# Block 2's norm behind the output projection: sums taken inside the projection, one low part on VectorE

## What is computed

```
mix = concat([a_out, b_out]) @ w_o[i]
x   = layer_norm(ALPHA * x + mix, ln1_g[i], ln1_b[i])      # the norm of this case
gate, up = split(x @ w_ffn_in[i], 2)
ple = (p[i] @ w_ple[i]) * sigmoid(x @ w_ple_gate[i])
...
def layer_norm(x, g, b):
    mu  = mean(x, -1)
    var = mean(square(x - mu), -1)
    return (x - mu) * rsqrt(var + 1e-5) * g + b
```

## Time and profile before

| | |
|---|---|
| median of 3 runs | 2500.24 us (2498.78 to 2500.97) |
| the profiled execution, its own time | 2500.13 us |
| its span, first to last instruction | 2498.3 us |
| mean granted TensorE clock | 0.992 of full |
| PE busy | 2424.8 us, 97% of the span |
| PE weight loads busy | 2033.0 us, 81% |
| DVE busy | 1765.1 us, 71% |
| ACT busy | 1095.0 us, 44% |
| POOL busy | 1065.5 us, 43% |
| chain that ended last | PE 75%, DVE 10%, issue 5%, ACT 4%, POOL 3%, DMA 3% |

### The profile page before, as it was taken

One profiled execution on the slowest core, in us unless ns is written; L12 is line 12 of the kernel. 1 busy time (PEld: TensorE's weight loads), 2 busy tenths in 40 slices (PEclk: granted clock), 3 DMA queues, 4 the chain that ended last, 5 costly groups with the idle time before them and its releaser, 6 DMA issues.

```text
span 2498.3 us, 35167 instructions
## 1 busy us (share of the span) xinstructions
PE 2424.8 (97%) x13615; PEld 2033.0 (81%) x13615; DVE 1765.1 (71%) x2671; ACT 1095.0 (44%) x1803; POOL 1065.5 (43%) x600
## 2 busy tenths in 40 slices
PE   6999999999999999999999999999999999999997
PEld 4777788988777788998777779999877777999985
DVE  4677777864477787774597478887468747888746
ACT  4325532434426543443444555444444355444442
POOL 0323553434234244544254446544515534755441
PEclk8999999999999999999999999999999999999998
DMA  8613345553322433332232113332223212333221
GB/s 288 203 51 123 114 152 169 189 164 110 95 85 85 135 118 119 102 102 85 86 85 76 55 64 127 108 104 92 95 82 85 76 51 68 102 124 105 94 87 49
DMA packets 239645, 268.87 MB, mean 108 GB/s; under 512 B 19976, under 2 KB 204024, under 8 KB 239224
## 3 DMA queue, kind: packets, MB, share of 16 engines
q1 hardware_dynamic: 239480, 266.63, 33.1%
HBM read 264.51 MB, written 2.10 MB: 107 GB/s over the span
## 4 chain that ended last, share of the span: by engine, by line
PE 75%; DVE 10%; issue 5%; ACT 4%; POOL 3%; DMA 3%; SPq 1%; ACTq 0%; DVEq 0%; POOLq 0%
PE bank L2801 22%; PE bank L2803 22%; PE bank L2802 22%; DVE k_lo L2057 1%; DMA raw<-in_w_ffn_in 1%; DVE r L1908 1%; POOL w_lo L1652 1%; POOL k_lo L1663 1%; DMA raw<-in_ffn_w 1%; ACT k_hi L1105 1%; DVE u_sum L2074 1%; PE bank L3404 1%; PE bank L3470 1%; DVE u_t_raw L2087 1%; PE bank L3130 1%
## 5 line engine op out<-in xcount | busy, mean ns | idle before, releaser
L1663 POOL TENSOR_TENSOR k_lo<-raw,k_hi 128x512 fp32r<-128x512 f32 x297 | 430.0, 1459 | 542.9 <-ACT k_hi L1105 541.9
L1652 POOL TENSOR_TENSOR w_lo<-raw,w_hi 128x2048 fp32r<-128x2048 f32 x53 | 248.8, 4694 | 525.3 <-ACT w_hi L1051 446.3
L1105 ACT ACTIVATE k_hi<-raw 128x512 fp32r<-128x512 f32 x444 | 270.9, 626 | 310.7 <-PE bank L2803 249.4
L2801 PE MATMUL bank<-h_hi,k_lo 128*128 128x256 f32 (+1 forms) x1156 | 370.8, 321 | 3.8 <-DVE k_lo L2057 2.5
L2802 PE MATMUL bank<-h_lo,k_hi 128*128 128x256 f32 (+1 forms) x1156 | 369.6, 320 | 0.0
L2803 PE MATMUL bank<-h_hi,k_hi 128*128 128x256 f32 (+1 forms) x1156 | 369.5, 320 | 0.0
L2801 PE MATMUL bank<-h_hi,w_lo 128*128 128x512 f32 x800 | 325.0, 406 | 10.7 <-DVE h_lo L2017 3.9
L2803 PE MATMUL bank<-h_hi,w_hi 128*128 128x512 f32 x800 | 313.4, 392 | 0.0
L2802 PE MATMUL bank<-h_lo,w_hi 128*128 128x512 f32 x800 | 313.3, 392 | 0.0
L2801 PE MATMUL bank<-f_hi,k_lo 128*128 128x512 f32 x704 | 278.4, 395 | 8.6 <-DVE u_row L2118 2.9
L2801 PE MATMUL bank<-u_t_hi,k_lo 128*128 128x256 f32 x1008 | 282.6, 280 | 1.2 <-POOL k_lo L1663 1.2
(11 more groups left out here) (401 smaller groups left out, 4929.6 us busy)
## 6 DMA issues: line engine op xcount, KB each, us to landing
raw<-in_ffn_w SPq DMA_DIRECT2D x56, 1024.0 KB, 5.4
raw<-in_w_ffn_in SPq DMA_DIRECT2D x44, 1024.0 KB, 5.1
raw<-in_w_in SPq DMA_DIRECT2D x34, 1024.0 KB
b_raw<-in_ada_w SPq DMA_DIRECT2D x32, 1024.0 KB, 5.2
f_raw<-in_w_ffn_out SPq DMA_DIRECT2D x24, 512.0 KB, 3.4
z_a<-in_ada_w SPq DMA_DIRECT2D x4, 2048.0 KB, 14.1
g_raw<-in_ada_w SPq DMA_DIRECT2D x8, 1024.0 KB, 5.6
raw<-in_w_out SPq DMA_DIRECT2D x8, 1024.0 KB
```

The lines of the kernel that those rows point to most:

```text
L1105: act.activation(hi, src, ACT.Copy).then_inc(s.f_hi.up, 1)
L1652: pool.tensor_tensor(b.w_lo[p][:, 0:n], b.raw[p][:, 0:n], b.w_hi[p][:, 0:n].bitcast(F32), ALU.subtract)\
L1663: pool.tensor_tensor(lo, src, hi.bitcast(F32), ALU.subtract).then_inc(s.f_lo.up, 1)
L2801: pe.matmul(out, wlo, xhi, start=start, stop=False)
```

## The change

- Inside `attended(0)`, behind its first k, PE sums tiles 0 and 1 of x over the width into bank 6: two f32 matmuls. DVE (`dve_early_shift`) then subtracts this sum over 256 from all eight tiles, before the projection is added to them. What is left is a small mean.
- ACT squares tiles 0 to 6 as they become ready (`act_square_out`), ahead of its split(15); DVE squares tile 7. PE sums the squares of tiles 0 to 3 into bank 7 inside `attended(1)`, ahead of output tile 7, and those of tiles 4 to 6 at the start of `pe_layer_norm`. Then come the two sums of x as before, and the square of tile 7.
- The variance is now the mean of squares minus the square of the remaining mean: ACT squares bank 6, DVE subtracts (signal `s.var`). ACT's logarithm and exponential follow.
- Weight unit 15's low part moves from POOL to DVE, behind that subtraction.
- DVE takes the remaining mean off tiles 0 and 1 before the multiplications and off tiles 2 to 7 between them.
- The dummy matmuls ahead of `lay.pair(7)` are 8 in place of 19. Elsewhere they stay 19.

```diff
 def act_layer_norm(act, e, l):
-    for k in range(KD):
-        act.wait_ge(*s.ld(l, k + 1))
-        act.activation(b.sq[:, k, :], b.x[:, k, :], ACT.Square).then_inc(s.lsq.up, 1)
     act.wait_ge(*s.lmean(l, 2))
-    act.activation(b.r[:, :], bank[7][:, :], ACT.Ln, bias=b.eps[:, 1:2], scale=1.0 / D).then_inc(s.l_r.up, 1)
-    act.wait_ge(*s.l_r(l, 1))
+    act.activation(b.sq[:, 1, :], bank[6][:, :], ACT.Square, scale=1.0 / D).then_inc(s.l_r.up, 1)
+    act.wait_ge(*s.var(l, 1))
+    act.activation(b.r[:, :], b.sq[:, 1, :], ACT.Ln, bias=b.eps[:, 1:2]).then_inc(s.l_r.up, 1)
+    act.wait_ge(*s.l_r(l, 2))
     act.activation(b.r[:, :], b.r[:, :], ACT.Exp, scale=-0.5).then_inc(s.l_r.up, 1)
+def act_square_out(act, e, l, ks):
+    for k in ks:
+        act.wait_ge(*s.res(l, k + 1))
+        act.activation(b.sq[:, k, :], b.x[:, k, :], ACT.Square).then_inc(s.lsq.up, 1)
@@ ACT's program
     split(14)
+    act_square_out(act, e, l, range(KD - 1))
     split(15)
@@ POOL's program
     split(14)
-    split(15)
@@ DVE's program
-def dve_layer_norm(dve, e, l):
-    dve.wait_ge(*s.lmean(l, 1))
-    for k in range(KD):
-        dve.scalar_tensor_tensor(b.x[:, k, :], bank[6][:, :], -1.0 / D, b.x[:, k, :], ALU.mult, ALU.add)\
-           .then_inc(s.ld.up, 1)
-    dve.wait_ge(*s.l_r(l, 2))
+def dve_layer_norm(dve, e, lay, l):
+    dve.wait_ge(*s.res(l, KD))
+    dve.tensor_tensor(b.sq[:, KD - 1, :], b.x[:, KD - 1, :], b.x[:, KD - 1, :], ALU.mult).then_inc(s.lsum.up, 1)
+    dve.wait_ge(*s.l_r(l, 1))
+    dve.wait_ge(*s.lmean(l, 3))
+    dve.scalar_tensor_tensor(b.sq[:, 1, :], bank[7][:, :], 1.0 / D, b.sq[:, 1, :], ALU.mult, ALU.subtract)\
+       .then_inc(s.var.up, 1)
+    dve_split(dve, e, lay.pair(7))
+    for k in range(2):
+        dve_less_mean(dve, e, k, -1.0 / D)
+    dve.wait_ge(*s.l_r(l, 3))
     for k in range(KD):
-        dve.wait_ge(*s.ld(l, k + 1))
+        dve.wait_ge(*s.ld(l, KD + k + 1))
         dve_scaled(dve, e, k)
         if k == 0:
             dve_normed(dve, e, l * 2, 0)
+        if k + 2 < KD:
+            dve_less_mean(dve, e, k + 2, -1.0 / D)
         if k == 1:
             dve_normed_low(dve, e, l * 2, 0)
+def dve_early_shift(dve, e, lay, l):
+    dve.wait_ge(*s.lmean(l, 1))
+    for k in range(KD):
+        dve.wait_ge(*lay.bank_out(k % 2, PART_USE[k]))
+        dve_less_mean(dve, e, k, -1.0 / (2 * P))
@@ PE's program
 def pe_layer_norm(pe, e, l):
+    pe_square_sums(pe, e, l, range(4, KD - 1))
     pe.wait_ge(*s.lsum(l, 6))
+    pe.wait_ge(*s.ld(l, KD))
     pe.matmul(bank[6][:, :], b.ones[:, :], b.r[:, :], start=True, stop=False)
     pe.wait_ge(*s.res(l, KD))
     pe.matmul(bank[6][:, :], b.ones[:, :], b.x[:, KD - 1, :], start=False, stop=True).then_inc(s.lmean.up, 1)
-    for k in range(KD):
+    pe.wait_ge(*s.lsum(l, 7))
+    pe.matmul(bank[7][:, :], b.ones[:, :], b.sq[:, KD - 1, :], start=False, stop=True).then_inc(s.lmean.up, 1)
+def pe_square_sums(pe, e, l, ks):
+    for k in ks:
         pe.wait_ge(*s.lsq(l, k + 1))
-        op = pe.matmul(bank[7][:, :], b.ones[:, :], b.sq[:, k, :], start=(k == 0), stop=(k == KD - 1))
-    op.then_inc(s.lmean.up, 1)
+        pe.matmul(e.bank[7][:, :], b.ones[:, :], b.sq[:, k, :], start=(k == 0), stop=False)
@@ attended(0), inside the loop over k
+                if k == 0:
+                    for n in range(2):
+                        pe.wait_ge(*lay.bank_out(n, PART_USE[n]))
+                        op = pe.matmul(bank[6][:, :], b.ones[:, :], b.x[:, n, :], start=(n == 0), stop=(n == 1))
+                    op.then_inc(s.lmean.up, 1)
@@ attended(1), inside the loop over m
+                if m == 6:
+                    pe_square_sums(pe, e, l, range(4))
@@ the first pair of products behind the norm
-                  + [(bank[2], s.res(l, 4)), (bank[3], s.res(l, 4))])
+                  + [(bank[2], s.res(l, 4)), (bank[3], s.res(l, 4))], busy=BUSY_SHIFTED)
```

More of the change, by code:

```diff
@@ L32 @@
 NB = T // P
-BUSY = 19
+BUSY, BUSY_SHIFTED = 19, 8
 G = 256
@@ L590, in __init__ @@
         self.mh, self.mh2 = in_turn("mh_mh2", 8, 8)
-        self.gn_sq, self.lsq = in_turn("gn_sq_lsq", 2, 8)
+        self.gn_sq, self.lsq = in_turn("gn_sq_lsq", 2, 7)
         self.cn_sq, self.is_relu = in_turn("cn_sq_is_relu", 2, 9)
@@ L598, in __init__ @@
         self.gn_m, self.v_m = in_turn("gn_m_v_m", 2, 1)
-        self.gn_x, self.lsum = in_turn("gn_x_lsum", 2, 6)
+        self.gn_x, self.lsum = in_turn("gn_x_lsum", 2, 7)
         self.cn_x, self.wi = in_turn("cn_x_wi", 2, 1)
@@ L639, in __init__ @@
         self.v_n = up("v_n", 4)
-        self.lmean = up("lmean", 2)
-        self.ld = up("ld", 8)
-        self.l_r = up("l_r", 2)
+        self.lmean = up("lmean", 3)
+        self.ld = up("ld", 2 * KD)
+        self.l_r = up("l_r", 3)
         self.n2_sum = up("n2_sum", 3 + 6)
@@ L646, in __init__ @@
         self.n2_r = up("n2_r", 3)
-        self.n2_var = up("n2_var", 1)
+        self.var = up("var", 2)
         self.lxr = up("lxr", KD + 1)
@@ L2445, in dve_layer_norm, with dve_less_mean @@
     dve_normed_low(dve, e, l * 2, KD - 1)
+def dve_less_mean(dve, e, k, part):
+    s, b = e.s, e.b
+    dve.scalar_tensor_tensor(b.x[:, k, :], e.bank[6][:, :], part, b.x[:, k, :], ALU.mult, ALU.add)\
+       .then_inc(s.ld.up, 1)
+def dve_early_shift(dve, e, lay, l):
+    s, b = e.s, e.b
+    dve.wait_ge(*s.lmean(l, 1))
+    for k in range(KD):
+        dve.wait_ge(*lay.bank_out(k % 2, PART_USE[k]))
+        dve_less_mean(dve, e, k, -1.0 / (2 * P))
 def dve_scaled(dve, e, k):
@@ L2542, in dve_shift_norm @@
     dve.scalar_tensor_tensor(b.f_full[:, 1, :], bank[7][:, :], 1.0 / D, b.f_full[:, 1, :], ALU.mult, ALU.subtract)\
-       .then_inc(s.n2_var.up, 1)
+       .then_inc(s.var.up, 1)
     for k in range(2):
@@ L2743, in dve_layer2 @@
     c = l * 2
+    dve_early_shift(dve, e, lay, l)
     for k in range(KD):
+        dve.wait_ge(*s.ld(l, k + 1))
         dve.wait_ge(*(s.att(l, 3 * (k // 4) + k % 4 + 1) if k % 4 < 3 else
                       s.tile(lay.pair(6), k // 4, 1)))
-        dve.wait_ge(*lay.bank_out(k % 2, PART_USE[k]))
         dve.tensor_tensor(b.x[:, k, :], b.x[:, k, :], bank[OUT2_BANK[k]][:, :], ALU.add).then_inc(s.res.up, 1)
@@ L2750, in dve_layer2 @@
             dve_add_up(dve, e, l, k)
-    dve_layer_norm(dve, e, l)
+    dve_layer_norm(dve, e, lay, l)
     x = quarters(b.x)
@@ L2836, in pe_unit_at, with keep_busy, pe_first_pair @@
             between()
-def keep_busy(pe, e, out):
+def keep_busy(pe, e, out, n=BUSY):
     eye = e.b.eye_r[:, :].unsqueeze(1).to_broadcast([P, NB, P])
-    for _ in range(BUSY):
+    for _ in range(n):
         pe.matmul(out[:, :].rearrange("p (a c) -> p a c", a=NB), e.b.eye_r[:, :], eye, start=True, stop=True)
-def pe_first_pair(pe, e, u, ready, outs, rows=P, between=None, busy=True):
+def pe_first_pair(pe, e, u, ready, outs, rows=P, between=None, busy=BUSY):
     s, b = e.s, e.b
@@ L2863, in pe_first_pair @@
     if busy:
-        keep_busy(pe, e, outs[0][0])
+        keep_busy(pe, e, outs[0][0], busy)
     for k in range(KD):
@@ L3214, in pe_layer1 @@
                   [(bank[m], lay.bank_free(m, 0)) for m in range(2)] + [(bank[2], None), (bank[3], None)],
-                  between=later if l == 0 else None, busy=l > 0)
+                  between=later if l == 0 else None, busy=BUSY if l else 0)
     pe.wait_ge(*s.par(l, 2))
```

4 lines of the change are left out of this document (3 added, 1 removed).

## The result

| | before | after |
|---|---|---|
| median, same comparison, 7 runs each | 2498.78 us (2494.62 to 2500.97) | 2508.07 us (2505.22 to 2510.25) |
| ratio after to before | | 1.0040, 95% interval 1.0030 to 1.0049 |
| the profiled execution's own time | 2500.13 us | 2508.07 us |
| its span | 2498.3 us | 2506.3 us |
| PE busy | 2424.8 us | 2427.0 us |

The change makes the kernel slower by 7.5 to 12.2 us. The forecast was 8.7 us slower, 2509.0 us.

A forecast was written before the change was run, and what follows sets the result against it. PE, busy 97%, was taken to bound the kernel, each norm being a chain whose delay carries to the end. 3.39 + 0.97 = 4.36 a layer, 8.7 for two, on 2500.24 gives 2509.0 us; range 2504.5 to 2512.5.

The forecast's parts named there:

- Term 1: Projection: six f32 sums at 0.86 are paid in full, moving its end (E) by 5.14 us a layer.
- Term 2: Norm, from the projection's end (E): six more f32 sums take 5.14 us, so DVE's variance starts at E + 5.34.
- Term 3: DVE behind the variance: subtraction, low part, two mean subtractions, 4.02 us; first multiplication E + 9.36, low part making it 2.0 late.
- Term 4: From first multiplication to first product 3.73 us: first product at E + 13.09, 3.39 us later a layer than before.
- Term 5: Products behind the norm: second k starts 3.01 us behind the first, where nine products need 2.04; loss 0.97 a layer.
- Term 6: PE's gaps in the norm may bring half clock; taken as nothing because dummies absorb it, 1.6 kept for the range.
- Rival (b): Half clock on products or a further stall: 0.6 to 1.6 us a layer more, 2510.5 to 2512.5 us; chance 0.12.
- Rival (c): DVE's low part covered, 2505.0 us, or sums falling into projection waits, 2498.7 with all six; chance 0.15 together.
- Rival (d): An f32 sum costs much less than 0.86 us; at 0.227 it gains 3.2 a layer, 2493.8 us; chance 0.05.

The follow-up runs named there:

- e1: Kernel before plus six f32 sums in each layer's projection whose result is unused; 2509.81 us, 1.0037 to 1.0061 of before.
- e7: Kernel after redesigned: one rounded early sum, rounded squares all behind the projection, low part on POOL, 21 dummies; 2490.06 us, 0.9964 to 0.9985 of before.
- e3: Kernel after with DVE's low part of unit 15 ahead of its wait for the variance, and 19 dummies; 2503.94 us, 1.0020 to 1.0044 of before.
- e6: Kernel after with unit 15's low part back on POOL and 19 dummies; 2502.81 us, 1.0016 to 1.0039 of before.
- e9: Kernel after with its eight squares, and the ones that sum them, rounded (fp32r); 2499.46 us, 0.9994 to 1.0012 of before.
- e11: Kernel before with rounded squares, 16 dummies, and more dummies in PE's pauses ahead of and between their sums; 2492.80 us, 0.9975 to 0.9993 of before.
- e8: Same redesign as e7 but every sum in f32, mean taken off four tiles ahead of the variance; 2500.54 us, 1.0007 to 1.0026 of before.
- e12: e7 with four sums of squares ahead of the sum of the running total; 2486.94 us, 0.9945 to 0.9972 of before.

## Why the prediction was right, point by point

- The number: the medians of the comparison are 9.3 us apart, against 8.7 forecast. That the forecast of 2509.0 lies only 0.9 from the measured 2508.07 is in part luck, since the kernel before was 1.5 faster in this comparison than the 2500.24 it was added to.
- Term 1, six sums, 5.14: measured 5.24 after, 5.21 in e1. Right; none of them fell into a wait. Two sums amid products took 1.71 in the rows it rested on, and 1.72 in e1.
- The side remark that DVE's stalled addition stays at 4.28 was off: it is 5.13 after, since DVE and POOL meet at another point. It held nobody in the kernel after, as stated; in e7 it made the running sum late.
- Term 2, the variance at E + 5.34: measured E + 5.41.
- Term 3, the first multiplication at E + 9.36, 2.0 of it for the low part: measured E + 9.42. e3 and e6 give 1.85 for the low part.
- Term 4, first product at E + 13.09: measured 13.14 in both layers.
- Term 5, second k 3.01 behind the first: 3.00 in the second layer. In the first it is 3.75, with the half clock in it. The third k loses 0.15 more (5.19 behind the first product, before 4.08), which the term had at nothing.
- Term 6, the clock at nothing: this is the term that was mis-sized. It cost 0.60 by the third k, in one layer of two. The reason given, that the dummies stand where the half clock would be served, held in the second layer only. Rival (b) put 0.6 to 1.6 a layer on it; it was there in one layer of the profiled execution, at the low end. Added up, 5.24 - 1.70 + 1.11 is 4.65 without it and 5.25 with it; the layer is longer by 5.21. Two layers with one such loss make 9.9 us, and the ratio gives 7.5 to 12.2.
- Rival (c), a covered low part: e3 and e6 build it. It was worked out as 2.4 a layer slower than before (4.36 - 2.0); their layers are 2.75 and 2.78 longer, since the low part gave back 1.85 and the third k lost its 0.15. Their times, 2503.9 and 2502.8, can't be set beside the 2505.0 worked out there, because the kernel before was faster in their comparisons. In the kernel after, the order of the code excluded it, as argued. Its second half, sums that fall into waits, is excluded by e1.
- Rival (d): its arithmetic for a cheap f32 sum was too kind. It let the norm shrink with every sum. With eight of the twelve at 0.23 it would give 4.36 - 8 x 0.63, a gain of 0.7 a layer; e9 gains 0.28. Its variance is at E + 3.23, where 5.34 less four sums' saving would be 2.8: ACT, which squares the mean behind its own split, sets it by then. On the price itself the rows decided rightly, and the measurement, 0.86 a sum, is against the page that is cited there, which makes no difference by type. The 216 ns of that section of the Trainium skill are its gap of a single matmul by itself; for a stream it gives about 131 ns, and the trace's 227 is near the first. Another page of the Trainium skill, "FP8 and Floating Point Precision", section "TensorE Precision Notes", says that true FP32 takes four passes. As an estimate from that page, four product distances are 0.91, near the 0.86 measured; weighing it would have spoken against (d).

## What to carry to other kernels

Where one engine is busy all the time, moving its work earlier hides nothing: a step is only cheaper if it is dropped, is made in fewer passes, or falls into a wait that a view shows. Count passes, not calls: here a sum in plain f32 cost nearly four times one with rounded operands, and rounding the squares was worth 2.4 to 5 us a layer (e11, e9, and e7 against e8), and no reordering tried here more than 1.9 (e3, e6, e12). And whenever an operation with two SBUF inputs moves on DVE, look for POOL's long operations near its new place: here a lead or lag of some hundredths of a microsecond decided over 2 us.
